# Second mixer of a two-stack layer: who computes the long convolution's last taps, who splits the weights, and where the layer-norm mean is taken

## The reference

```python
proj = hn @ w_in[l]
xv, bg, cg, ga, gg = jnp.split(proj, splits, axis=-1)      # each 512 wide
y_sc = bg * causal_depthwise_conv_2(cg * xv, w_conv)         # 3 taps
u = a * jax.nn.sigmoid(gate)                                # a = ga, gate = gg
u = causal_depthwise_conv_2(u, w_dw) + b_dw                 # 31 taps
y_cf = jax.nn.silu(layer_norm(u, ln_g, ln_b))
y = jnp.concatenate([rms_norm_2(y_sc, ...), rms_norm_2(y_cf, ...)], axis=-1)
h = h + y @ w_out[l]
```

## Time and profile before

| what | value |
| --- | --- |
| median of 3 runs | 1417.63 us (1415.38 to 1417.72) |
| the profiled execution, its own time | 1414.53 us |
| its span in the profile | 1412.7 us |
| PE busy | 1349.1 us (95%) |
| DVE busy | 880.3 us (62%) |
| ACT busy | 787.4 us (56%) |
| POOL busy | 413.2 us (29%) |
| mean granted TensorE clock | 0.982 |

### The profile page before, as it was taken

One profiled execution on the slowest core, in us unless ns is written; L12 is line 12 of the kernel. 1 busy time (PEld: TensorE's weight loads), 2 busy tenths in 40 slices (PEclk: granted clock), 3 DMA queues, 4 the chain that ended last, 5 costly groups with the idle time before them and its releaser, 6 DMA issues.

```text
span 1412.7 us, 26186 instructions
## 1 busy us (share of the span) xinstructions
PE 1349.1 (95%) x8936; PEld 1231.0 (87%) x8936; DVE 880.3 (62%) x1675; ACT 787.4 (56%) x1407; POOL 413.2 (29%) x244
## 2 busy tenths in 40 slices
PE   7999989999998857999999999999999999999997
PEld 7998969988978855999999999999998888888885
DVE  4787357656677785589991455666635555555555
ACT  6546255444456524457777666676745555555554
POOL 0101310000013831028988766666650000000001
PEclk9999999999999988999999999999999999999999
...
GB/s 298 153 117 120 1 90 195 187 191 192 185 163 131 132 94 103 135 153 179 190 189 182 165 138 147 136 149 135 148 170 189 188 183 193 183 189 190 183 191 119
DMA packets 62025, 225.16 MB, mean 159 GB/s; under 512 B 7153, under 2 KB 7537, under 8 KB 61569
## 3 DMA queue, kind: packets, MB, share of 16 engines
...
HBM read 223.12 MB, written 1.05 MB: 159 GB/s over the span
## 4 chain that ended last, share of the span: by engine, by line
PE 90%; DVE 4%; POOL 2%; issue 1%; ACT 1%; DMA 0%; POOLq 0%; ACTq 0%; DVEq 0%
PE bank L506 78%; PE bank L969 4%; POOL arena L1521 1%; DVE arena L1942 1%; PE bank L579 1%; PE bank L707 1%; PE bank L486 1%; PE bank L717 1%; PE bank L715 1%; PE bank L533 1%; ACT arena L1021 1%; PE bank L922 1%; DMA consts<-in_consts 0%; PE bank L729 0%; DVE arena L2008 0%
## 5 line engine op out<-in xcount | busy, mean ns | idle before, releaser
L1051 ACT ACTIVATE w_hi<-ring 128x1024 fp32r<-128x1024 f32 x414 | 438.6, 1060 | 510.5 <-PE bank L506 341.4
L1594 DVE TENSOR_TENSOR w_lo<-ring,w_hi 128x1024 fp32r<-128x1024 f32 x274 | 337.1, 1230 | 297.5 <-ACT w_hi L1051 295.0
L506 PE MATMUL bank<-hT_hi,w_hi 128*128 128x256 f32 (+2 forms) x1728 | 432.2, 288 | 3.2 <-ACT w_hi L1051 1.1
L506 PE MATMUL bank<-hT_lo,w_hi 128*128 128x256 f32 (+2 forms) x1728 | 423.1, 283 | 0.0
L1548 POOL TENSOR_TENSOR w_lo<-ring,w_hi 128x1024 fp32r<-128x1024 f32 x128 | 310.6, 2428 | 172.9 <-ACT w_hi L1051 172.7
L506 PEld LDWEIGHTS bank<-hT_hi,w_hi 128*128 128x128 f32 x1728 | 327.6, 190 | 6.7 <-ACT w_hi L1051 2.7
L506 PEld LDWEIGHTS bank<-hT_lo,w_hi 128*128 128x128 f32 x1728 | 328.6, 190 | 0.2
L506 PE MATMUL bank<-hT_hi,w_lo 128*128 128x256 f32 (+2 forms) x1728 | 240.9, 282 | 4.3 <-POOL w_lo L1530 4.3
L506 PEld LDWEIGHTS bank<-hT_hi,w_lo 128*128 128x128 f32 x1728 | 221.0, 190 | 4.7 <-POOL w_lo L1530 4.7
L506 PE MATMUL bank<-w_hi,wgt_hi 128*128 128x512 f32 x504 | 199.9, 397 | 0.0
L506 PE MATMUL bank<-w_hi,wgt_lo 128*128 128x512 f32 x504 | 199.4, 396 | 0.0
...
## 6 DMA issues: line engine op xcount, KB each, us to landing
ring<-in_stream SPq DMA_DIRECT2D x414, 512.0 KB, 3.2
...
```

The lines of the kernel that those rows point to most:

```text
L506: mm = nc.tensor.matmul(o, a, b, start=first and not low_part and xp is x[0], stop=last and low_part)
L1051: nc.scalar.activation(w_hi[:, g % S, :], ring[:, g % R, :], ACT.Copy).then_inc(hi_done, 1)
L1594: nc.vector.tensor_tensor(w_lo[:, g % S, :], ring[:, g % R, :], w_hi[:, g % S, :].bitcast(F32), ALU.subtract).then_inc(lo_done, 1)
```

## The change

1. In blocks 2 and 3 VectorE adds taps 1 to 22 and TensorE the last 8 of each: 16 fp32 matmuls of a diagonal 128x128 matrix (`tap_diag`, a tap's 128 factors on the diagonal) with a shifted `upad`, accumulated in bank 7, two behind each of in2 tiles 8 to 15. `merge(2)` and `merge(3)` add bank 7 to `cfacc`. VectorE does all taps of blocks 0 and 1. ScalarE's products and GpSimd's adds are gone. GpSimd writes the diagonal matrices early, behind `inv_rms(2)`.
2. GpSimd splits in2 tiles 2 to 19 and out2 tiles 0, 2, 3, 4, 5; VectorE out2 tile 1 and from 6 on.
3. cg * xv stays in the PSUM bank of xv, and the three short taps read it there. in2 results use three banks (4, 5, 6) instead of four.
4. All taps are added before the last short mixer block. The column sums come before in2 tile 19 and the sum of squares right behind it.

```diff
-SHARED = (17, 18)
-PROD = 4
+DVE_TAPS = (CF_TAPS, CF_TAPS, 23, 23)
...
+        taken[0] = 20992
+        tap_diag = area(2 * (CF_TAPS - DVE_TAPS[2]), P)
...
+            def last_conv_taps(b, k0, n):
+
+                pe.wait_ge(u_sb, b - 1)
+                for k in range(k0, k0 + n):
+                    mm = nc.tensor.matmul(bank[7][:, (b - 2) * T:(b - 1) * T],
+                                          tap_diag[:, (b - 2) * (CF_TAPS - DVE_TAPS[2]) + k - DVE_TAPS[b], :],
+                                          upad[:, b - 2, k:k + T], start=False, stop=(b == 3 and k == CF_TAPS - 1))
+                return mm
...
+
+                w = tile(G_IN2 + m)
+                if m >= 3:
+                    taken_in2(m - 3)
+                off, width = (0, META + T) if m < 8 else (META, T) if (m - 8) % 3 == 2 else (META - 2, T + 2)
+                out_block(w, bank[4 + m % 3][:, 0:width], slice(off, off + width), 4 if m == 0 else None)
...
+            for m in range(8):
+                in2_tile(m)
+            nc.tensor.matmul(bank[7][:, :], zb, zb.unsqueeze(1).to_broadcast([P, HALF // P, P]), start=True, stop=False)
+            pe.wait_ge(tap_diag_done, 1)
+            for m in range(8, 16):
+                in2_tile(m)
+                b = 2 + (m - 8) // 4
+                mm = last_conv_taps(b, DVE_TAPS[b] + 2 * ((m - 8) % 4), 2)
+                if m % 4 == 3:
+                    mm.then_inc(last_taps, 1)
+            for m in range(16, 19):
+                in2_tile(m)
+            pe.wait_ge(cf_done, NH)
+            column_sums(mean, cfacc, range(NH)).then_inc(mean_full, 1)
+            in2_tile(19)
+            pe.wait_ge(cen_sq, NH)
+            token_sums(var, sq2).then_inc(var_full, 1)
             for b in range(NH):
-                taken_in2(16 + b)
-            pe.wait_ge(cf_done, 2)
-            column_sums(mean, cfacc, (0, 1))
+                pe.wait_ge(bg_out, b + 1)
             pe.wait_ge(yT_ready, 1)
             out2_tile(0, 4)
-            pe.wait_ge(cf_done, NH)
-            column_sums(mean, cfacc, (2, 3)).then_inc(mean_full, 1)
+            pe.wait_ge(var_diag_done, 1)
+            nc.tensor.matmul(rstd_row, ones, var_diag, start=True, stop=True).then_inc(rs_act, 1)
             pe.wait_ge(yT_ready, 2)
             out2_tile(1, 4)
             pe.wait_ge(sc_sq, NH)
+            pe.wait_ge(rms_out, 1)
...
-            def product(b, k):
-
-                n = products[0]
-                if n >= PROD:
-                    act.wait_ge(pool_tap, n - PROD + 1)
-                nc.scalar.activation(prod[:, n % PROD, :], upad[:, b, k:k + T], ACT.Copy,
-                                     scale=col("cf_conv", b * CF_TAPS + k)).then_inc(prod_out, 1)
-                products[0] += 1
-
-            products = [0]
...
+                else:
+                    act.wait_ge(u_out, b + 1)
+                    nc.scalar.activation(cfacc[:, b, :], u_bank[b][:, 0:T], ACT.Identity,
+                                         scale=col("cf_conv", b * CF_TAPS), bias=col("cf_b", b)).then_inc(first_tap, 1)
...
-                his(G_IN2 + m + 2, 1)
+                if b < NH - 1:
+                    his(G_IN2 + m + 2, 1)
+            for b in range(NH):
+                act.wait_ge(cen_out, b + 1)
+                nc.scalar.activation(sq2[:, b, :], cfacc[:, b, :], ACT.Square).then_inc(cen_sq, 1)
+            his(G_IN2 + 19, 1)
             act.wait_ge(bg_out, NH)
             gained(3, scacc, "on_sc")
             nc.scalar.activation(sq_sc[:, 3, :], scacc[:, 3, :], ACT.Square).then_inc(sc_sq, 1)
+            nc.scalar.activation(rms2[:, 12:13], eps_col, ACT.Silu)
             his(G_OUT2, 1)
-            for b in range(NH):
-                act.wait_ge(cen_out, b + 1)
...
-            his(G_OUT2 + 1, 2)
-            his(G_OUT2 + 3, 1)
...
+                if b % 2:
+                    for q in (b - 1, b):
+                        act.wait_ge(ln_silu, q + 1)
+                        gained(NH + q, cfacc, "on_cf")
+                    his(G_OUT2 + 1 + b // 2, 1)
             for b in range(NH):
                 nc.scalar.activation(sq2[:, b, :], cfacc[:, b, :], ACT.Square).then_inc(y_sq, 1)
+            his(G_OUT2 + 3, 1)
...
+                if n == 2:
+                    for b in (2, 3):
+                        for k in range(DVE_TAPS[b], CF_TAPS):
+                            ins = nc.gpsimd.tensor_scalar(tap_diag[:, (b - 2) * (CF_TAPS - DVE_TAPS[2]) + k - DVE_TAPS[b], :],
+                                                          ident, col("cf_conv", b * CF_TAPS + k), None, ALU.mult)
+                    ins.then_inc(tap_diag_done, 1)
...
-            pool_taps(0, CF_TAPS - SHARED[0])
-            pool_taps(1, 8)
-            split(G_IN2 + 8 + S)
-            pool_taps(1, CF_TAPS - SHARED[1] - 8)
-            for g in range(G_IN2 + 9 + S, G_OUT2 + S):
+            for g in range(G_IN2 + S, G_OUT2 + 1):
                 split(g)
-            for n, rms, r in ((1, rms_sc, r_sc), (2, ms_cf, rstd_cf), (3, rms_cf, r_cf)):
+
+            def inverse_root(n, r, rms):
+
                 pool.wait_ge(rms_out, n)
                 nc.gpsimd.tensor_tensor(r, rms, neghalf[:, 0:NT], ALU.pow).then_inc(rms_done, 1)
+
+            inverse_root(1, rstd_cf, ms_cf)
+            split(G_OUT2 + 2)
+            split(G_OUT2 + 3)
+            inverse_root(2, r_sc, rms_sc)
+            split(G_OUT2 + 4)
+            split(G_OUT2 + 5)
+            inverse_root(3, r_cf, rms_cf)
...
-                if b < 2:
-                    nc.vector.tensor_tensor(upad[:, b, 14:UPAD], src, sgate[:, b % 2, :], ALU.mult)
+                if b >= 2:
+                    nc.vector.tensor_tensor(upad[:, b - 2, 14:UPAD], src, sgate[:, b % 2, :], ALU.mult).then_inc(u_sb, 1)
                 nc.vector.tensor_tensor(u_bank[b][:, 14:UPAD], src, sgate[:, b % 2, :], ALU.mult).then_inc(u_out, 1)
...
-            ends = [SHARED[0], SHARED[1], CF_TAPS, CF_TAPS]
+            ends = DVE_TAPS
...
-                dve.wait_ge(pool_tap, SHARED_AT[b] + CF_TAPS - SHARED[b])
-                nc.vector.tensor_tensor(cfacc[:, b, :], cfacc[:, b, :], pacc[:, b, :], ALU.add).then_inc(cf_done, 1)
+                dve.wait_ge(last_taps, b - 1)
+                nc.vector.tensor_tensor(cfacc[:, b, :], cfacc[:, b, :], bank[7][:, (b - 2) * T:(b - 1) * T], ALU.add)\
+                    .then_inc(cf_done, 1)
...
-            los(G_IN2, 2)
             gate_block(0)
-            los(G_IN2 + 2, 1)
-            taps(4, (0,))
-            los(G_IN2 + 3, 1)
+            taps(10, (0,))
             gate_block(1)
-            taps(4, (0,))
-            los(G_IN2 + 4, 1)
-            taps(4, (0, 1))
-            los(G_IN2 + 5, 1)
+            taps(11, (0, 1))
             gate_block(2)
-            taps(4, (0, 1))
-            los(G_IN2 + 6, 1)
-            taps(4, (0, 1, 2))
-            los(G_IN2 + 7, 1)
+            taps(11, (0, 1, 2))
             gate_block(3)
...
-                taps(6, range(NH))
+                if b < NH - 1:
+                    taps(13 if b == 0 else 15, range(NH))
+                else:
+                    taps(2 * CF_TAPS, range(NH))
+                    merge(2)
+                    merge(3)
+                xv = bank[4 + (m + 1) % 3]
                 dve.wait_ge(tiles_done, G_IN2 + m + 2)
                 dve.wait_ge(cg_out, b + 1)
-                nc.vector.tensor_tensor(mconv[:, b % 2, :], bank[4 + (m + 1) % 4][:, 0:T + 2], cgs[:, b % 2, 0:T + 2],
...
+                w = COLS["sc_conv"] + b * SC_TAPS
+                for k in range(SC_TAPS):
                     done = steps[0]
                     taps(2, range(NH))
                     dve.wait_ge(dve_step, done)
-                    nc.vector.scalar_tensor_tensor(scacc[:, b, :], mconv[:, b % 2, k:k + T], cols[:, w + k:w + k + 1],
-                                                   scacc[:, b, :], ALU.mult, ALU.add).then_inc(dve_step, 1)
...
+                    if k == 0:
+                        ins = nc.vector.tensor_scalar(scacc[:, b, :], xv[:, 0:T], cols[:, w:w + 1], None, ALU.mult)
+                    else:
+                        ins = nc.vector.scalar_tensor_tensor(scacc[:, b, :], xv[:, k:k + T], cols[:, w + k:w + k + 1],
+                                                             scacc[:, b, :], ALU.mult, ALU.add)
...
                 if b:
                     low_part(b - 1, scacc, "on_sc")
-                taps(3, range(NH))
-                dve.wait_ge(dve_step, done)
+                if b == NH - 1:
+                    dve.wait_ge(mean_full, 1)
+                    for q in range(NH):
+                        nc.vector.scalar_tensor_tensor(cfacc[:, q, :], bank[0][:, 0:T], -1.0 / HALF, cfacc[:, q, :],
+                                                       ALU.mult, ALU.add).then_inc(cen_out, 1)
+                dve.wait_ge(m_out, b + 1)
...
-                if b == 1:
-                    taps(2 * (ends[0] - next_tap[0]), (0, 3))
-                    merge(0)
```

(51 more changed lines are left out.)

66 lines of the change are left out of this document (9 added, 57 removed).

## The result

The median is 1390.43 us (1389.55 to 1394.56, 4 runs) against 1416.93 (1415.38 to 1417.72, 4 runs) of the kernel before: ratio 0.9821, 95% interval 0.9809 to 0.9833 (ratios are taken over all runs, so they are not exactly the quotient of the two medians). The forecast was 1395.5 and 1389 to 1403. The profiled execution took 1389.55 us, 25.0 less than the 1414.53 of the one before.

A forecast was written before the change was run, and what follows sets the result against it. TensorE was taken as the bound, waiting mainly for VectorE. `closing_rows` 24.6 us earlier, less clock 1.5, handovers 0.9 and diagonal matrices 0.3, left 21.9 gained: 1417.63 - 21.9 = 1395.7, rounded to 1395.5 us; range 1389 to 1403.

The forecast's parts named there:

- What bounds the kernel, and what the change removes: Second mixer: TensorE, 90% of the chain, waits 13.5 us for VectorE's product by bg; forecast to become 2.0.
- TensorE's own time: Up to the mean: tile 7 ends at 462.4, 16 added matmuls take 6.9 us, tile 18 ends at 501.0.
- VectorE's time, the low parts: Before the mean: two low parts each wait 0 to 2.4 us for GpSimd's split, 2.4 together; VectorE done at 502.8.
- Clock 1.5: Behind the expected 2 us wait at the mean: 0 to 4 us lost to 1.2 GHz, taken as 1.5.
- Handovers 0.9: Six waits between engines that now lie close, 0.15 us each, 0.9 us taken off the gain.
- diagonal matrices 0.3: GpSimd writing 16 matrices at 213: at most 6.4 us, covered; delay to VectorE's instructions beside them taken as 0.3.
- The cross-check: Waits of PE of 22.3 us become 2.0, matmuls of 7.2 added: 13.1 gained; the other 11.5 must be clock.
- the second rival: At the mean, VectorE is in time and TensorE waits for nothing: 26.6 us gained, 1391; chance 0.08.
- The likeliest case: Column sums at about 503 after a 2.0 us TensorE wait; 19 to 26 us gained, chance 0.64.
- The first: Rival: before the mean VectorE stays further behind and the clock falls; 14.8 us gained, some 1403; chance 0.18.
- The third: Rival: GpSimd's splits come late and TensorE waits at second passes; 12 to 15 us gained, 1404; chance 0.06.
- The fourth: Rival: every VectorE instruction waits for running GpSimd splits; `closing_rows` 10.4 us later, 1428; chance 0.04.

## Why the prediction was right, and where it was mis-sized

**What bounds the kernel, and what the change removes: right.** VectorE's lateness at the mean went from 13.5 us to 0.3. The parts taken back one at a time cost 8.3 (splits), 5.8 (short taps in PSUM), 5.6 (taps on TensorE) and 4.9 (mean): 24.6, near the stage's 25.7. That they add up so well is no proof of independence: each was taken back with the rest in place, each holds 1.5 to 3.5 us of clock, and the 5.6 holds the 1.1 of a low part that met a split.

**TensorE's own time: right.** Tile 7 ended at 462.67 (462.4), clearing took 0.23 (0.25), two taps 0.86 with a new matrix each, and tile 18 ended at 501.37 (501.0). From the column sums to `closing_rows` it took 29.72 (29.4); 0.3 of that is column sums of 1.99 instead of 1.7.

**VectorE's time, the low parts: mis-sized.** "I take the middle, 2.4 for both" became 0. Both began just ahead of a split:

```profile
495.81 0.47 DVE L1969 SCALAR_TENSOR_TENSOR yT_lo<-arena,cols,yT_hi 128x256 fp32r<-128x256 f32 x1
```

(the changed kernel's DVE) and, on its POOL,

```profile
492.22 2.40 POOL L1520 TENSOR_TENSOR w_lo<-ring,w_hi 128x1024 fp32r<-128x1024 f32 x1 [1.35 <-ACT w_hi L1071]
495.95 2.60 POOL L1520 TENSOR_TENSOR w_lo<-ring,w_hi 128x1024 fp32r<-128x1024 f32 x1 [1.33 <-ACT w_hi L1071]
```

The low part fell into the 1.3 us that GpSimd was idle, which the prediction denied ("GpSimd splits without pause"): in tiles 8 to 15 TensorE takes 3.73 us per tile with its two taps, a split 2.4. The prediction had both numbers (2.87 + 0.86, and 2.40). But that both low parts began 0.13 to 0.14 us ahead of a split, and not behind one, was luck; nothing in the prediction foresaw it. That the price is real was shown by their neighbours: 1.97 with 8 taps, 1.53 with none, and 2.39 with 12, the upper end of the range. The other way, VectorE's waits for tiles 9, 12 and 15 were 0.23 + 0.92 + 0.63 = 1.8 instead of 0.8. Together VectorE ended 1.2 before the forecast 502.8, and the column sums came at 501.64 instead of 503.0.

**"Clock 1.5": 0 here.** With a wait of 0.3 no stretch fell below 1.00. For the 2.0 us wait that I expected, 1.5 would have been little: the experiments paid 3.5 us behind a wait of 2.0, near the upper end of my 0 to 4, 1.7 behind 1.8 and 2.0 behind 5.6. The term was wrong because the wait under it was.

**"Handovers 0.9" and "diagonal matrices 0.3": 0 and 0.** Between the column sums and `closing_rows` the only loss is the 0.3 of slower column sums. The diagonals took 1.0 us each, not the 0.40 at most that I had bounded from a copy of 256 columns:

```profile
213.81 16.00 POOL L1511 TENSOR_SCALAR arena<-consts,cols 128x128 f32<-128x128 f32 x16
```

The bound was wrong by 2.5 times: it came from another kind of operation. It cost next to nothing on the path (the mixer began 0.1 us later than before), because nothing waited for them until 462 and VectorE's instructions beside them went on. A split from SBUF took 1.21 as always; two normalisations took 1.03 instead of 0.88, an addition 0.51 instead of 0.42, a cast 0.42 instead of 0.29.

**The sum.** Earlier column sums 1.36, clock 1.5, handovers 0.9 less the 0.3 by which the part behind them took longer than 29.4, diagonals 0.3: 3.7, the same 3.7 by which the gain at `closing_rows` (556.98 - 531.36 = 25.6) passed 21.9. The medians gained 0.9 more, within the spread of runs. All four terms erred to the same side, so the time lies near the lower end of the range. The cross-check was off as well: of the waits of PE before it left out 1.1 us for ScalarE's high part and 0.9 for VectorE's cg * xv, so what it calls clock, 11.5, is 9.5 at most.

**The rivals.** In mechanism and size this is the second rival, "VectorE is in time" (26.6 gained, 1391), to which I gave 0.08, because it "needs low parts that meet no split"; that condition held. The likeliest case named the same steps with a lateness of 2.0; its 19 to 26 gained holds the profiled 25.0 but not the medians' 26.5. The first was seen only in experiments (1394 to 1400 there). The third did not come: PE waited for no split of GpSimd, and none before the mean took over 2.62. The fourth is excluded: the long taps of alternating blocks ran at 0.40 beside splits. Its rule (the Trainium skill, "Perfetto Trace Analysis", Optimizing Scalar/DVE Operations) holds here for a part of VectorE's work: taps with an input in PSUM never waited, while short taps and low parts with only SBUF inputs did and took up to 2.39 us.
